# Three projections of a two-layer decoder as three passes over high and low parts

## The chip, the cores and the metric

One core of a Trainium2 chip runs the whole program in one launch. Its engines are TensorE (PE, matrix products), VectorE (DVE), ScalarE (ACT), GpSimd (POOL) and SyncE (SP, which here issues the weight loads); each works off its own instructions in order and waits for the others on semaphores. The metric is the time of one execution on the device, in microseconds (us).

## The reference

Two layers of a causal decoder are computed for 256 prompt tokens and 8 sample tokens (264 columns together), of width 1024, in fp32. What matters here is the head of layer 0:

```python
h = rmsnorm(x, P['norm_mix_pre'][l])
u, v, z, xbc, dt = jnp.split(h @ w_in, SPLIT0, axis=-1)     # widths 1024, 1024, 1024, 1536, 16
u = jax.nn.gelu(u)
v = layernorm(jax.nn.gelu(v), a_ln_g, a_ln_b)
xbc, conv_new = causal_dwconv(xbc, conv0, conv_w, conv_b)   # depthwise, 4 taps
xbc = jax.nn.silu(xbc)
dtf = jax.nn.softplus(dt.astype(f32) + dt_bias.astype(f32))
yb = group_rmsnorm(y * jax.nn.silu(z), b_norm, B_GROUPS)    # y: the scan over xbc with dtf
```

After it come the scan, a spatial gate, the output projection, cross-attention, a dense SwiGLU; then layer 1 with a gated recurrence, cross-attention and eight experts.

## The kernel before

The tokens lie transposed in memory: eight chunks of 128 features by 264 columns (`HT` after a norm). A projection multiplies strips of 512 weight columns; each strip comes in two blocks of four chunks of 128 rows (1 MB), and gives four tiles of 128 outputs by 264 tokens. Blocks are loaded by SyncE (L428 to L433) in the order of the `weights` calls (L350 to L371: xbc, dt, v, z, u, out0, k0, q0 and so on) into a ring of two slots (`RING`); the load of block b waits until block b - 2 is given free. dt has two small blocks of 16 columns.

There are two kinds of projection. The plain one (`project`, L696) multiplies fp32 weights straight from the slot (L712). The split one (`project_split`, L724) takes weights in quarters (two chunks by 512 columns). ScalarE writes a quarter's rounded high part (`make_hi`, L1295), VectorE the rest, its low part (`make_lo`, L1612), both into a ring of four (`QRING`); TensorE then makes three passes: high by high, high by low, low by high (L742 to L744). The tokens have two parts as well: ScalarE writes the high one (`input_hi`, L1316), VectorE the low one within `finish_norm` (L1648 to L1652), for the norms named in `SPLIT_NORMS`. A plain block is free when TensorE has used it, a split one when the low parts of its two quarters are made (L341). A place in the ring of four is free when TensorE has used the quarter.

When the parts are made is set by the order of the instructions on ScalarE and VectorE. Before either takes a finished tile n (`tile`, L1311 on ScalarE and L1628 on VectorE; `copied`, L1633), it makes the parts that tile n needs and up to three (ScalarE) or two (VectorE) quarters beyond:

```python
            goal = needed(n)
            while goal < min(needed(n) + lead, len(quarters)):
                old = quarters[goal][0] - RING
                if old >= 0 and blocks[old][4] is not None and blocks[old][4] > n:
                    break
                goal += 1
            return range(made, max(made, goal))
```

The break is for a quarter whose slot is still held by a plain block. `first_hi`, `first_lo` and `lo_through` make parts at fixed points instead. Four banks take the results in turn, so a new tile waits until the tile four before it is taken out (`take`, L682).

The order on the engines at the head: SyncE loads tokens, parameters and states, then the blocks. TensorE turns the tokens (eight tiles xT), then the parameters and the convolution's state, sums the squares, and goes on with xbc (12 tiles), dt, v (8 tiles), transposes of the convolved xbc, z (8 tiles), the scan. ScalarE squares and copies the eight xT tiles (L1345), makes the root (L1350, `root`), a sigmoid and an exponential of parameters (L1352, L1354), copies xbc's tiles out (L1357), makes an exponential for dt (L1360), waits for VectorE's dt chain, writes two more (L1362), and only then takes v's tiles (L1366); SiLU of xbc (L1369) follows, then z (L1382). VectorE does the norm (`finish_norm(0)`), then the convolution in three groups of four tiles (L1674 to L1696), each when its tiles are out, then a long chain of small operations for dt (L1701 to L1719), and the scan.

Of the kernel before, what the change touches and what calls it, by code (L numbers as in the profile page):

```python
# [21 lines left out]
D = 1024  # L22
DC = D // P
# [39 lines left out]
STEPS_MAX = 3 * NE  # L63


SPLIT = {"q0", "q1", "f", "q", "i", "g"} | {f"{kind}{i}" for kind in ("gate", "up") for i in range(6)}
SPLIT_NORMS = (2, 4, 6, 8)
BIG = 1e30


def program(nc, a, o):
    h_rows = nc.dram_tensor("h_rows", [T, D], F32, kind="Internal").ap()
    oe_rows = nc.dram_tensor("expert_rows", [(STEPS_MAX + 1) * P, D], F32, kind="Internal").ap()
    with ExitStack() as ctx:
# [6 lines left out]
        def S(name):  # L81

            if name not in made:
                made[name] = ctx.enter_context(nc.semaphore(name))
            return made[name]
# [211 lines left out]
        def n_of(name, i=0):  # L297
            return first[name] + i
# [379 lines left out]
        def _(pe):  # L678
# [17 lines left out]
            def project(name, rhs, kchunks, cols, between=None, norm=None):  # L696


                n = n_of(name)
                for c0 in range(0, cols, SL):  # L700
                    width = min(SL, cols - c0)
                    nt = (width + P - 1) // P
                    for k0 in range(0, kchunks, KB):
                        w = next_block()
                        ks = min(KB, kchunks - k0)
                        for i in range(nt):
                            m = min(P, width - i * P)
                            b = take(n + i) if k0 == 0 else bank(n + i)
                            for k in range(ks):
                                if norm is not None and c0 == 0 and i == 0:  # L710
                                    wait_norm(norm, k0 + k + 1)
                                last = mm(b[0:m, 0:T], w[:, k, i * P:i * P + m], rhs[:, k0 + k, :],  # L712
                                          start=(k0 + k == 0), stop=(k0 + k == kchunks - 1))
                            if k0 + ks == kchunks:
                                last.then_inc(tile_done, 1)
                            elif i == nt - 1:
                                last.then_inc(part_used, 1)
                            if between is not None:
                                between()
                    n += nt  # L720
# [81 lines left out]
            pe.wait_ge(S("st_loaded"), 16)  # L802
            transposes(n_of("st"), [(st_in[:, c * P:(c + 1) * P], 24, P) for c in range(CC)])
            square_sums(0)
            project("xbc", HT, DC, CONV_CH, norm=0)
            project("dt", HT, DC, 16)
            project("v", HT, DC, D)

            n = n_of("tr0")
            for i in range(3):  # L810
# [35 lines left out]
            for c in range(DC):  # L846
                last = mm(ps[:, 5, 128 + 16 * c:144 + 16 * c], head_of[:, c * P:(c + 1) * P], exd, start=True, stop=True)
            last.then_inc(S("dt_tm_done"), 1)
            project("z", HT, DC, D)

            b = take(n_of("vmean"))
            pe.wait_ge(empty["a"], emptied(n_of("v", 7))[1])
# [438 lines left out]
        def _(act):  # L1291
# [43 lines left out]
            def root(k):  # L1335
                act.wait_ge(S("square_sums_done"), k + 1)
                f(rs, ps[:, 4, 0:T], ACT.Sqrt, bias=eps_c, scale=1.0 / D).then_inc(S("root_ready"), 1)  # L1337
# [7 lines left out]
            for c in range(DC):  # L1345
                b = tile(n_of("xT", c))
                f(MT[:, c, :], b[:, 0:T], ACT.Square).then_inc(S("squares_ready"), 1)
                f(XT[:, c, :], b[:, 0:T], ACT.Copy).then_inc(empty["a"], 1)
            act.wait_ge(S("eps_ready"), 1)
            root(0)  # L1350
            act.wait_ge(S("lb_diff"), 1)
            f(lb1, omlb, ACT.Sigmoid).then_inc(S("lb_ready"), 1)  # L1352
            act.wait_ge(S("small_loaded"), 64)
# [245 lines left out]
        def _(dve):  # L1599
# [38 lines left out]
            def finish_norm(k):  # L1638

                kind, layer, pre = NORMS[k]  # L1640
                dve.wait_ge(S("root_ready"), k + 1)
                link(v.reciprocal(rs, rs))  # L1642
                if pre:
                    for c in range(DC + 2):
                        if c < DC:
                            STT(out=HT[:, c, :], in0=XT[:, c, :], scalar=gain(kind, layer, c), in1=rs,
                                op0=ALU.mult, op1=ALU.mult).then_inc(S("normed"), 1)
                        if c >= 2 and k in SPLIT_NORMS:  # L1648

                            dve.wait_ge(S("x_hi_made"), DC * SPLIT_NORMS.index(k) + c - 1)  # L1650
                            TT(x_lo[:, c - 2, :], HT[:, c - 2, :], x_hi[:, c - 2, :].bitcast(F32), ALU.subtract) \  # L1651
                                .then_inc(S("x_lo_made"), 1)  # L1652
                else:
                    for c in range(DC + 1):
                        if c < DC:
                            STT(out=MT[:, c, :], in0=MT[:, c, :], scalar=gain(kind, layer, c), in1=rs,
                                op0=ALU.mult, op1=ALU.mult).then_inc(S("out_scaled"), 1)
                        if c:
                            dve.wait_ge(S("out_scaled"), DC * posts.index(k) + c)
                            TT(XT[:, c - 1, :], XT[:, c - 1, :], MT[:, c - 1, :], ALU.add).then_inc(S("x_updated"), 1)  # L1660
# [6 lines left out]
            b = tile(n_of("st"))  # L1667
            v.tensor_copy(raws[:, :, 0:3, :], b[:, 0:288].rearrange("p (c b k) -> p c k b", c=CC, b=NB)) \
                .then_inc(empty["v"], 1)
            finish_norm(0)  # L1670
            dve.wait_ge(S("lb_ready"), 1)
            link(TS(omlb, lb1, -1.0, 1.0, ALU.mult, ALU.add))

            for c4 in range(3):  # L1674
                dve.wait_ge(empty["a"], emptied(n_of("xbc", 4 * c4 + 3))[1])
                cc = range(4 * c4, 4 * c4 + 4)
                for c in cc:
                    last = TS(XBC[:, c, 0:TP], raw[:, c, 3:259], par[:, CW + 36 + c:CW + 37 + c], None, ALU.mult)
                link(last)
                for k in range(3):  # L1680
                    for c in cc:
                        last = STT(out=XBC[:, c, 0:TP], in0=raw[:, c, k:k + TP], scalar=par[:, CW + 12 * k + c:CW + 12 * k + c + 1],
                                   in1=XBC[:, c, 0:TP], op0=ALU.mult, op1=ALU.add)
                    link(last)

                xs = XBC[:, 4 * c4:4 * c4 + 4, TP:T]
                tmp = t2[:, 0, 0:32].rearrange("p (c b) -> p c b", c=4)
                for k in range(4):
                    w = par[:, CW + 12 * k + 4 * c4:CW + 12 * k + 4 * c4 + 4].unsqueeze(2).broadcast_to([P, 4, NB])
                    link(TT(tmp if k else xs, raws[:, 4 * c4:4 * c4 + 4, k, :], w, ALU.mult))  # L1690
                    if k:
                        ins = TT(xs, xs, tmp, ALU.add)
                        if k < 3:
                            link(ins)
                        else:
                            ins.then_inc(S("conv_ready"), 1)  # L1696
# [21 lines left out]
            dve.wait_ge(S("aexp_ready"), 1)  # L1718
            TS(dtr[1], dtr[0], aexp, -1.0, ALU.mult, ALU.mult).then_inc(S("dt_done"), 1)  # L1719

            dve.wait_ge(S("dt_tm_done"), 1)
            v.tensor_copy(small[:, 64:128], ps[:, 5, 0:64]).then_inc(S("dt_tm_ready"), 1)
            link(v.tensor_copy(exc.rearrange("p c k -> p (c k)"), ps[:, 5, 128:256]))
# [449 lines left out]
```

## Time and profile before

| what | us |
|---|---|
| median of three runs | 2319.28 |
| lowest and highest of them | 2318.39, 2330.17 |
| the profiled execution | 2322.26 |
| its span, first to last instruction | 2320.6 |
| TensorE busy in the span | 2115.5 (91%) |
| VectorE busy | 1404.0 (61%) |
| ScalarE busy | 1132.7 (49%) |

The times of single instructions come from the profiled execution, whose time is 2.98 us above the median. In the rows, PE is TensorE's matmuls, PEld its weight loads, DVE VectorE, ACT ScalarE, SPq SyncE's queue; L712 is line 712 of the kernel; "out<-in" names the memory written and read; "xN" is a count; in square brackets stands the idle time before the instruction and what ended it. A plain fp32 product of a 128x128 weight tile shows as two matmul records, each pass of a split one as one. A granted clock of 1.00 is 2.4 GHz, 0.50 is 1.2 GHz.

### The profile page before, as it was taken

Reading aid. Unit: us, or ns where it says so; the run is one execution under the profiler, and the core shown is the slowest. Engines: PE = TensorE matmul, PEld = TensorE weight load, DVE = VectorE, ACT = ScalarE, POOL = GpSimd, SP = SyncE. Lnnn points to the kernel's source line nnn. Section 1 sums busy time; section 2 is a strip of 40 time slices with the busy share of each in tenths; the row PEclk is TensorE's granted clock in tenths of the full one; section 3 lists DMA queues with packets and bytes.
Section 4 is the critical chain, followed back from the end, with each engine's and each line's share of the span. In section 5 each row is a group of like instructions: output and inputs, shape, how many; then the busy total and the mean of one; then the engine's idle time right before and its main releaser. Section 6 shows DMA issues by size and latency. Waiting matters only on the chain.

```text
span 2320.6 us, 28455 instructions
## 1 busy us (share of the span) xinstructions
PE 2115.5 (91%) x10176; PEld 1685.7 (73%) x10176; DVE 1404.0 (61%) x1979; ACT 1132.7 (49%) x1498; POOL 147.4 (6%) x174
## 2 busy tenths in 40 slices
PE   7888789998999877989898699999999999999993
PEld 6675576556998777746656588888888888888882
DVE  2427613423440335371441599999999999999994
ACT  2221213123430235202211478888888888888883
POOL 2002210010000000140010000000000000000001
PEclk9998699999999988769999799999999999999997
DMA  5423354552544464235471599999999999999992
GB/s 134 138 74 100 109 195 150 179 184 91 182 154 146 158 233 134 66 100 205 158 253 55 218 384 369 384 364 386 370 382 368 383 380 374 372 379 376 378 373 74
DMA packets 232760, 551.76 MB, mean 238 GB/s; under 512 B 10406, under 2 KB 13698, under 8 KB 232678
## 3 DMA queue, kind: packets, MB, share of 16 engines
q1 hardware_dynamic: 211246, 470.68, 56.6%
q0 software_dynamic: 21440, 80.07, 10.2%
q8 instruction: 50, 0.82, 0.1%
q14 instruction: 24, 0.20, 0.0%
HBM read 521.18 MB, written 29.62 MB: 237 GB/s over the span
## 4 chain that ended last, share of the span: by engine, by line
PE 79%; DVE 12%; DMA 4%; ACT 3%; issue 2%; POOL 1%; DVEq 0%; ACTq 0%; POOLq 0%
PE banks L712 14%; PE banks L1267 8%; PE banks L1269 8%; PE banks L1268 8%; PE banks L763 5%; PE banks L1260 4%; PE banks L1258 4%; PE banks L1259 4%; PE banks L742 3%; PE banks L743 3%; PE banks L744 3%; PE banks L1049 2%; PE banks L787 2%; PE banks L1017 1%; PE banks L1277 1%
## 5 line engine op out<-in xcount | busy, mean ns | idle before, releaser
L2131 DVE TENSOR_TENSOR weight_parts<-arena,weight_parts 128x1024 fp32r<-128x1024 f32 x672 | 799.5, 1222 | 64.8 <-ACT weight_parts L1567 32.9
L1567 ACT ACTIVATE weight_parts<-arena 128x1024 fp32r<-128x1024 f32 x672 | 702.0, 1062 | 140.1 <-PE banks L1269 89.3
L712 PE MATMUL banks<-arena 128*128 128x264 f32 (+1 forms) x1584 | 372.6, 398 | 19.6 <-DMA arena<-in_ev_w_out 5.1
L712 PEld LDWEIGHTS banks<-arena 128*128 128x128 f32 (+1 forms) x1584 | 308.4, 196 | 83.2 <-issue 9.7
L1267 PE MATMUL banks<-weight_parts,token_parts 128*128 128x512 f32 x896 | 355.9, 397 | 6.2 <-DVE weight_parts L2131 6.2
L1269 PE MATMUL banks<-weight_parts,token_parts 128*128 128x512 f32 x896 | 350.2, 391 | 0.0
L1268 PE MATMUL banks<-weight_parts,token_parts 128*128 128x512 f32 x896 | 349.4, 390 | 0.0
L742 PE MATMUL banks<-token_parts,weight_parts 128*128 128x264 f32 x736 | 218.3, 297 | 47.8 <-DVE token_parts L1651 17.1
L743 PE MATMUL banks<-token_parts,weight_parts 128*128 128x264 f32 x736 | 216.5, 294 | 0.0
L744 PE MATMUL banks<-token_parts,weight_parts 128*128 128x264 f32 x736 | 215.9, 293 | 0.0
L1617 DVE TENSOR_TENSOR weight_parts<-arena,weight_parts 128x1024 fp32r<-128x1024 f32 (+1 forms) x96 | 111.1, 1178 | 154.9 <-ACT weight_parts L1304 138.8
L1267 PEld LDWEIGHTS banks<-weight_parts,token_parts 128*128 128x128 f32 x896 | 168.6, 188 | 42.9 <-DVE weight_parts L2131 9.8
L1269 PEld LDWEIGHTS banks<-weight_parts,token_parts 128*128 128x128 f32 x896 | 168.5, 188 | 35.9
L1268 PEld LDWEIGHTS banks<-weight_parts,token_parts 128*128 128x128 f32 x896 | 168.8, 188 | 33.2
L742 PEld LDWEIGHTS banks<-token_parts,weight_parts 128*128 128x128 f32 x736 | 146.4, 199 | 50.9 <-DVE weight_parts L1617 27.5
L1258 PE MATMUL banks<-weight_parts,token_parts 128*128 128x512 f32 x448 | 175.8, 392 | 0.0
L1260 PE MATMUL banks<-weight_parts,token_parts 128*128 128x512 f32 x448 | 174.6, 390 | 0.0
L1259 PE MATMUL banks<-weight_parts,token_parts 128*128 128x512 f32 x448 | 174.4, 389 | 0.0
L1642 DVE RECIPROCAL arena<-arena 128x264 f32<-128x264 f32 x11 | 19.8, 1801 | 253.9 <-ACT arena L1337 253.6
L1304 ACT ACTIVATE weight_parts<-arena 128x1024 fp32r<-128x1024 f32 (+1 forms) x96 | 96.8, 1022 | 132.9 <-PE banks L744 86.9
L743 PEld LDWEIGHTS banks<-token_parts,weight_parts 128*128 128x128 f32 x736 | 146.3, 199 | 0.0
L744 PEld LDWEIGHTS banks<-token_parts,weight_parts 128*128 128x128 f32 x736 | 145.8, 198 | 0.0
(417 smaller groups left out, 2196.1 us busy)
## 6 DMA issues: line engine op xcount, KB each, us to landing
arena<-in_moe_w_gate SPq DMA_DIRECT2D x112, 1024.0 KB, 7.5
arena<-in_moe_w_up SPq DMA_DIRECT2D x112, 1024.0 KB, 7.8
arena<-in_moe_w_down SPq DMA_DIRECT2D x112, 1024.0 KB, 7.5
arena<-in_ev_w_in SPq DMA_DIRECT2D x18, 1024.0 KB, 5.0
arena<-in_cache_mem_k POOLq DMA_DIRECT2D x16, 1024.0 KB, 6.5
arena<-in_cache_mem_v POOLq DMA_DIRECT2D x16, 1024.0 KB, 7.0
arena<-in_od_w_in SPq DMA_DIRECT2D x16, 1024.0 KB, 5.7
arena<-in_ffn_w_gate SPq DMA_DIRECT2D x10, 1024.0 KB, 5.0
```

Of the source, the lines that this page charges most:

```text
L712: last = mm(b[0:m, 0:T], w[:, k, i * P:i * P + m], rhs[:, k0 + k, :], start=(k0 + k == 0), stop=(k0 + k == kchunks - 1))
L742: mm(b[:, 0:T], hi[:, part], x_hi[:, c, :], start=(c == 0), stop=False)
L743: mm(b[:, 0:T], hi[:, part], x_lo[:, c, :], start=False, stop=False)
L744: last = mm(b[:, 0:T], lo[:, part], x_hi[:, c, :], start=False, stop=(c == DC - 1))
L1258: mm(out, xh, hi[:, cols], start=(s == 0 and i == 0), stop=False)
L1259: mm(out, xh, lo[:, cols], start=False, stop=False)
L1260: last = mm(out, xl, hi[:, cols], start=False, stop=(s == NSL - 1 and i == 3))
L1267: mm(out, xh, hi[:, cols], start=(c == 0), stop=False)
L1268: mm(out, xh, lo[:, cols], start=False, stop=False)
L1269: last = mm(out, xl, hi[:, cols], start=False, stop=(c == DC - 1))
L1567: f(wr_[:, q % QRING, 0, :], quarter(q), ACT.Copy).then_inc(S("hi_made"), 1)
L2131: TT(wr_[:, q % QRING, 1, :], quarter(q), wr_[:, q % QRING, 0, :].bitcast(F32), ALU.subtract) \
```

## The change

xbc, v and z join the split projections (`SPLIT`), and the first norm joins the norms that give both parts (`SPLIT_NORMS`). TensorE calls `project_split` for the three. ScalarE calls `first_hi("xbc")` before the first root and `input_hi(0)` after it. VectorE calls `first_lo("xbc")` before the first norm, `copied` in place of the plain wait ahead of each convolution group, and `lo_through("v", 7, 2)` after dt's chain. dt and u stay plain. With xbc, v and z the list of quarters begins with 28 new ones: 12, 8 and 8, the first four of them in blocks 0 and 1.

```diff
--- before.py
+++ after.py
@@ -63,8 +63,8 @@
 STEPS_MAX = 3 * NE
 
 
-SPLIT = {"q0", "q1", "f", "q", "i", "g"} | {f"{kind}{i}" for kind in ("gate", "up") for i in range(6)}
-SPLIT_NORMS = (2, 4, 6, 8)
+SPLIT = {"xbc", "v", "z", "q0", "q1", "f", "q", "i", "g"} | {f"{kind}{i}" for kind in ("gate", "up") for i in range(6)}
+SPLIT_NORMS = (0, 2, 4, 6, 8)
 BIG = 1e30
 
 
@@ -802,9 +802,9 @@
             pe.wait_ge(S("st_loaded"), 16)
             transposes(n_of("st"), [(st_in[:, c * P:(c + 1) * P], 24, P) for c in range(CC)])
             square_sums(0)
-            project("xbc", HT, DC, CONV_CH, norm=0)
+            project_split("xbc", CONV_CH, norm=0)
             project("dt", HT, DC, 16)
-            project("v", HT, DC, D)
+            project_split("v", D)
 
             n = n_of("tr0")
             for i in range(3):
@@ -846,7 +846,7 @@
             for c in range(DC):
                 last = mm(ps[:, 5, 128 + 16 * c:144 + 16 * c], head_of[:, c * P:(c + 1) * P], exd, start=True, stop=True)
             last.then_inc(S("dt_tm_done"), 1)
-            project("z", HT, DC, D)
+            project_split("z", D)
 
             b = take(n_of("vmean"))
             pe.wait_ge(empty["a"], emptied(n_of("v", 7))[1])
@@ -1346,8 +1346,10 @@
                 b = tile(n_of("xT", c))
                 f(MT[:, c, :], b[:, 0:T], ACT.Square).then_inc(S("squares_ready"), 1)
                 f(XT[:, c, :], b[:, 0:T], ACT.Copy).then_inc(empty["a"], 1)
+            first_hi("xbc")
             act.wait_ge(S("eps_ready"), 1)
             root(0)
+            input_hi(0)
             act.wait_ge(S("lb_diff"), 1)
             f(lb1, omlb, ACT.Sigmoid).then_inc(S("lb_ready"), 1)
             act.wait_ge(S("small_loaded"), 64)
@@ -1667,12 +1669,13 @@
             b = tile(n_of("st"))
             v.tensor_copy(raws[:, :, 0:3, :], b[:, 0:288].rearrange("p (c b k) -> p c k b", c=CC, b=NB)) \
                 .then_inc(empty["v"], 1)
+            first_lo("xbc")
             finish_norm(0)
             dve.wait_ge(S("lb_ready"), 1)
             link(TS(omlb, lb1, -1.0, 1.0, ALU.mult, ALU.add))
 
             for c4 in range(3):
-                dve.wait_ge(empty["a"], emptied(n_of("xbc", 4 * c4 + 3))[1])
+                copied(n_of("xbc", 4 * c4 + 3))
                 cc = range(4 * c4, 4 * c4 + 4)
                 for c in cc:
                     last = TS(XBC[:, c, 0:TP], raw[:, c, 3:259], par[:, CW + 36 + c:CW + 37 + c], None, ALU.mult)
@@ -1718,6 +1721,7 @@
             dve.wait_ge(S("aexp_ready"), 1)
             TS(dtr[1], dtr[0], aexp, -1.0, ALU.mult, ALU.mult).then_inc(S("dt_done"), 1)
 
+            lo_through("v", 7, 2)
             dve.wait_ge(S("dt_tm_done"), 1)
             v.tensor_copy(small[:, 64:128], ps[:, 5, 0:64]).then_inc(S("dt_tm_ready"), 1)
             link(v.tensor_copy(exc.rearrange("p c k -> p (c k)"), ps[:, 5, 128:256]))
```

## Rows read from the trace of the kernel before

**Rows 1.** The page, part 4: the chain that ended last, by engine.

```profile
PE 79%; DVE 12%; DMA 4%; ACT 3%; issue 2%; POOL 1%; DVEq 0%; ACTq 0%; POOLq 0%
```

**Rows 2.** The chain in order of time, 0 to 420 us: start us, us, what.

```profile
22.48 1.28 ACT L1337
...
26.77 46.54 PE banks L712 x200
73.33 5.05 DMA arena<-in_ev_w_in
78.43 30.42 PE banks L712 x128
109.28 1.28 ACT L1369
...
123.28 28.68 PE banks L712 x128
```

**Rows 3.** ScalarE's timeline, 0 to 165 us: start, us, line, operation, count [idle before].

```profile
9.25 0.39 ACT L1347 ACTIVATE arena<-banks 128x264 f32<-128x264 f32 x1 [7.03 <-PE banks L778]
...
14.99 0.39 ACT L1347 ACTIVATE arena<-banks 128x264 f32<-128x264 f32 x1
...
24.28 1.28 ACT L1352 ACT_TABLE_LOAD   x1
...
71.45 0.38 ACT L1357 ACTIVATE arena<-banks 128x256 f32<-128x256 f32 x1 [1.33 <-PE banks L712]
...
89.82 0.21 ACT L1362 ACTIVATE arena<-arena 16x8 f32<-16x8 f32 x1 [8.21 <-DVE arena L1719]
```

**Rows 4.** Loads of L433: the first alone, then the first two.

```profile
DMA to landing us min/median/max: 5.1/5.1/5.1
...
L433 SPq DMA_DIRECT2D arena<-in_ev_w_in x2: 394/451/508, 8.0 to 8.4; - x2
...
DMA to landing us min/median/max: 5.1/11.4/17.7
```

**Rows 5.** Stretches: us, granted clock, share of DMA engines, GB/s.

```profile
13.00:21.70 8.70, 1.00 0.66 25
```

**Rows 6.** VectorE's timeline, 0 to 165 us.

```profile
71.94 1.14 DVE L1678 TENSOR_SCALAR arena<-arena 128x256 f32<-128x256 f32 x4 [6.40 <-ACT arena L1358]
...
79.70 0.18 DVE L1698 COPY arena<-arena 128x36 f32<-128x36 f32 x1
```

**Rows 7.** A norm that gives both parts (before q0): VectorE, TensorE, ScalarE, in time.

```profile
395.90 1.80 DVE L1642 RECIPROCAL arena<-arena 128x264 f32<-128x264 f32 x1
...
399.53 0.56 PE L742 MATMUL banks<-token_parts,weight_parts 128*128 128x264 f32 x1 [4.18 <-DVE token_parts L1651]
...
402.81 0.43 ACT L1320 ACTIVATE token_parts<-arena 128x264 fp32r<-128x264 f32 x1 [0.32 <-DVE arena L1646]
```

**Rows 8.** Parts of q0's weights: ScalarE's and VectorE's timelines.

```profile
403.14 2.94 ACT L1304 ACTIVATE weight_parts<-arena 128x1024 fp32r<-128x1024 f32 x3
...
404.22 3.49 DVE L1617 TENSOR_TENSOR weight_parts<-arena,weight_parts 128x1024 fp32r<-128x1024 f32 x3 [0.41 <-ACT weight_parts L1304]
```

**Rows 9.** ScalarE's timeline: the copies of q0's last four tiles, first and last.

```profile
422.93 0.39 ACT L1447 ACTIVATE arena<-banks 128x264 f32<-128x264 f32 x1 [8.10 <-PE banks L744]
...
425.12 0.39 ACT L1447 ACTIVATE arena<-banks 128x264 f32<-128x264 f32 x1 [0.34 <-PE banks L744]
```

**Rows 10.** Stretches: us, TensorE busy (x), granted clock, DMA share, GB/s.

```profile
75.40:78.40 3.00, 0.00 (x0) 1.00 1.05 383
78.40:80.00 1.60, 1.57 (x4) 0.50 1.15 324
80.00:82.00 2.00, 2.00 (x7) 0.55 1.05 385
```

**Rows 11.** The page, part 5: weight loads of a split line; busy us, mean ns.

```profile
L742 PEld LDWEIGHTS banks<-token_parts,weight_parts 128*128 128x128 f32 x736 | 146.4, 199 | 50.9 <-DVE weight_parts L1617 27.5
```

**Rows 12.** The page, part 6: DMA issues of a line, KB, us to landing.

```profile
arena<-in_moe_w_gate SPq DMA_DIRECT2D x112, 1024.0 KB, 7.5
```

## Prediction

> **What bounds the kernel now.** I began with the shares of the chain that ended last: TensorE has 79% of the span, so a matmul that gets shorter is worth looking at [rows 1]. Then the same chain in order of time, over the stretch that the change touches [rows 2]: nearly all of 26.77 to 151.96 us is L712, the plain fp32 projections. xbc runs from 26.77 to about 71.45, when ScalarE takes its last tile [rows 3]; dt follows, then the load that ends at 78.38 [rows 2]; v takes 30.42 us and z 28.68 us. The stage is TensorE's, with VectorE and ScalarE largely idle beside it. So the question is whether these two, which now must make every weight's two parts, do it in time. Their queues are in order, and I read the order from the code.
>
> **The matmul itself: a gain.** z's 64 products (8 tiles of 8 chunks) took 28.68 us, 0.448 each [rows 2]. In the projections that are split already, four tiles end within 422.93 to 425.12 us, so a tile's last six matmuls (two chunks, three passes) take 0.73 us [rows 9], and a quarter of a weight strip (two chunks by 512 columns), 24 matmuls, takes 2.92 us. xbc, v and z are 12, 8 and 8 quarters: 28 x 2.92 = 81.8 us, against 44.7 (26.77 to 71.45) + 30.4 + 28.7 = 103.8 now. Alone that is 22 us of gain. A rule speaks against it: the Trainium skill (Perfetto Trace Analysis, Identifying the Most-Contended Engine) judges TensorE by the time of its weight loads and not of its matmuls. If loads were the bound, three at the 199 ns that a load is shown with [rows 11] make 0.60 us a product, and 224 products would lose 33 us; but three passes fit in 0.365 us [rows 9], so the loads overlap and I keep the matmuls' rate.
>
> **The start: +17.4 us.** The ScalarE helper that takes a finished tile (`tile`, L1311) first makes the high parts of up to three quarters beyond those needed (`ahead_of`, L377). Before the change the first quarters belonged to q0, whose ring slot is held by an earlier plain block, and the loop broke off. Now the first three belong to blocks 0 and 1, no block was before them, and ScalarE makes all three before its very first square; the `first_hi` that the change adds then finds nothing left. Block 0 lands 5.1 us after 8.0, at 13.1; the largest of the first two landings is 17.7, so block 1, issued at 8.4, lands at 26.1 [rows 4]. Between 13 and 21.7 us the queues moved 25 GB/s [rows 5]. Quarter 2 lies in block 1, so its conversion (1.06 us on ScalarE) ends at 27.2, and behind it wait all squares and copies of the tokens, the root and the table loads. The first square now stands at 9.25, the last at 14.99 [rows 3]. TensorE has four transposed tiles ready (four banks), the other four follow at 0.82 us each (14.99 - 9.25 over seven) from 27.9, when the first bank is free: the last is turned at 31.2, 16.2 later than now. The rest up to the root is TensorE's own and moves along: root's table load at 38.7 instead of 22.48 [rows 2]. The norm then also gives the low part: where it is already done so, TensorE starts 3.63 us after the reciprocal's start [rows 7]; so root (1.8 with its table: ScalarE is at its next table load at 24.28 [rows 3]), then 40.5 + 3.63 = 44.15 instead of 26.77.
>
> **xbc: +7.3 us.** ScalarE's high part takes 1.06 (2.94 for three), VectorE's low part 1.2 (3.49 for three) [rows 8]. Each strip of four tiles adds a convolution of 7.8 us on VectorE (71.94 to 79.70) [rows 6], in which no low part is made. Working through it: ScalarE ends the token parts 7.3 us after the reciprocal began (402.81 + 0.43 against 395.90) [rows 7], then come two table loads of 1.28 with an operation each (3.0; the first is shown [rows 3]): quarter 3's parts are ready at 51.9 and 53.1. Quarters 0 to 3 run 44.15 to 57.5, with 1.7 us for a clock that starts low: after the 3 us gap of now, 75.4 to 78.4, 0.50 was granted and then 0.55 until 82, the lower level of 1.2 GHz [rows 10], and 3.6 us at half speed lose some 1.7. SyncE now reloads a slot on the low parts' count: block 3 goes out at 53.1 and lands 5.05 later [rows 2] at 58.2. ScalarE asks for its first half (quarter 6) before it empties the first tile, so that bank is free at 59.8 and not right after the tile, at 55.9. Quarters 4 and 5 run 59.8 to 66.8 (1.2 for the clock). The fourth tile is out at 61.25, the convolution ends at 69.05, the low part of quarter 6 at 70.25: 3.5 us of idle, then 6 and 7 until 77.85 (again 1.7). Block 5 goes out on quarter 7's low part, 71.4, and lands at 76.45; quarters 8 and 9 run 78.05 to 83.9. The second convolution, 79.5 to 87.3, puts quarter 10's low part at 88.5: 10 and 11 run 88.55 to 96.1. That is 51.95 us where 44.68 were.
>
> **dt and the wait before v: +14.0 us.** dt stays plain and takes 3.9 us as now (71.45 to 75.4, where TensorE falls idle [rows 10]): 96.1 to 100. The look-ahead stops at dt's plain blocks, so ScalarE first makes a high part of v after it has written dt's exponentials, for which it waits on VectorE: third convolution, then the dt chain. From the third convolution's start at 71.94 [rows 6] to ScalarE's going on behind the chain at 89.82 [rows 3] are 17.9 us now. TensorE doesn't wait for it there, only for v's load. After: 96.6 + 17.9 = 114.5, two short operations 0.3, high part 1.06, low part 1.2: v starts at 117.1 instead of 78.43. What is late next, were this gone, is v's block (issued when half of dt is done, 98, landed 103), so the load is hidden.
>
> **v and z: -5.3 and -5.3 us.** v's eight quarters: 23.4 plus 1.7 for the clock, 25.1 against 30.4. The conversions stay ahead: 1.2 of VectorE and 1.06 of ScalarE to 2.92 of TensorE, and the blocks go out two quarters earlier than they are used. Between v and z (the SiLU of the convolution, transposes, 109.28 to 123.28 [rows 2]) nothing changes. z's first two quarters are made during v; 23.4 against 28.7. u is plain and its loads go out earlier. GpSimd's queue waits for the same events as now.
>
> **Sum.** 17.4 + 7.3 + 14.0 - 5.3 - 5.3 = +28.1 us. The profiled execution took 2322.26 us (span 2320.6), 2.98 above the median of 2319.28; so it would be 2350.4 for such an execution and **2347** for the median.
>
> **Bounds.** Block 1's landing: one load's time (5.05) after block 0, at 18.2, gives back 7.9 us; at 15.2, when ScalarE has made the first two quarters, the most, 10.9; block 2, which now goes out at 16.5, can push it to the end of the burst, some 2 us later. I take 26.1, since block 2 is behind it in one queue. The loads on the path (blocks 3 and 5): 5.05 to the 7.5 us of the expert weights [rows 12], +5. The clock: no loss after the three gaps within xbc (-4.6) or twice the loss (+4.6). Token parts and table loads are rows of their own and move little.
>
> **Rivals.**
> 1. The cover holds: every low part is ready when TensorE asks. It decides at the point where VectorE's low part of quarters 6, 10 and 12 comes before the quarter ahead has ended, and it needs ScalarE not to stand still at the start. Then 103.8 becomes 81.8, and only the norm costs 1.1 (1.8 + 3.63 where 22.48 to 26.77 is 4.29 now): 2298. For it: VectorE and ScalarE have the time in total. Against: the order of their queues. Chance 0.03. The Trainium skill (FP8 and Floating Point Precision, TensorE Precision Notes) has true fp32 as four passes, so three would save a quarter, an estimate of 26 us of 103.8; the trace doesn't quite agree, 0.365 to 0.448 is 19%.
> 2. Block 1 is not late, since the slow interval of 13 to 21.7 moves: +18 instead of +28, 2337. For it: it is one interval of one execution. Against: the small loads that fill it are issued as before. 0.12.
> 3. As 2, and the stalls in xbc are half of mine: 2319 + 28 - 10 - 6 = 2331 or less, about the edge of no change. 0.05.
> 4. The loads on the path at 7.5 us, clock low for longer: 2358 to 2364. 0.12.
> 5. Weight loads bind, as the rule has it: 33 us lost and 22 not gained in the matmuls, partly in time that is idle in the forecast: from 2347 to some 2390. 0.02.
>
> The forecast has the remaining 0.66, at 2341 to 2356.
>
> **How the numbers follow.** Rival 2 and the lower end of rival 4 belong in the range: 2334 to 2359; outside are 1, 3, 5 and the upper part of 4, below 0.2. 0.5% is 11.6 us, about what a measurement of this kernel can tell from no change: faster (under 2307.7) 0.03, within 0.5% 0.05, slower 0.92.
>
> **What would show it.** In the changed profile: ScalarE's first instructions are three of L1304, the third waiting until about 26 us for a load, and the first square behind them. The first split matmul near 44. In xbc two idle times of TensorE before L742 that end on VectorE's L1617, each after a convolution (L1682). A gap of some 17 us after dt, closed by the chain L1714, ScalarE's exponentials, L1304, L1617. v in about 25 us, z in about 23.4, and everything after z as it was, 28 us later. If the first square is still near 9 us, the first step is wrong; if TensorE goes on to v before dt's exponentials are written, the third is.

## The result, and the profile after

| what | before | after |
|---|---|---|
| median, us | 2318.84 (4 runs, 2315.7 to 2330.17) | 2343.86 (4 runs, 2341.69 to 2349.34) |
| the profiled execution, us | 2322.26 | 2341.69 |
| its span, us | 2320.6 | 2340.1 |

The ratio is 1.0103, with a 95% interval of 1.0064 to 1.0141: 25 us slower, where the forecast was 28 (2347, range 2334 to 2359). TensorE's share of the chain that ended last fell from 79% [rows 1] to 75%: its matmuls did get shorter, and other engines took their place on the path. The interval is wide, 14.8 to 32.7 us. Line numbers of after lie up to four above those of before, and those of the experiments up to some seven higher still.

ScalarE's timeline of after, 0 to 165 us: start, us, line, operation, count, and in brackets the idle time before it and what ended it ("..." stands for lines left out).

```profile
13.11 2.00 ACT L1304 ACTIVATE weight_parts<-arena 128x1024 fp32r<-128x1024 f32 x2 [10.90 <-DMA arena<-in_ev_w_in]
25.32 1.06 ACT L1304 ACTIVATE weight_parts<-arena 128x1024 fp32r<-128x1024 f32 x1 [10.20 <-DMA arena<-in_ev_w_in]
26.28 0.37 ACT L1347 ACTIVATE arena<-banks 128x264 f32<-128x264 f32 x1
...
94.90 0.38 ACT L1359 ACTIVATE arena<-banks 128x256 f32<-128x256 f32 x1 [0.27 <-PE banks L744]
...
113.26 0.21 ACT L1364 ACTIVATE arena<-arena 16x8 f32<-16x8 f32 x1 [8.21 <-DVE arena L1722]
113.48 3.88 ACT L1304 ACTIVATE weight_parts<-arena 128x1024 fp32r<-128x1024 f32 x4
```

ScalarE's first work is three high parts (L1304). The third stands still for 10.20 us until block 1 lands at 25.3, and the first square, at 9.25 before [rows 3], comes behind it at 26.28. At the other end, the first high part of v waits for the exponential at 113.26.

TensorE's timeline of after, the entries that begin with an idle time, from the first split matmul to the scan.

```profile
43.71 0.56 PE L742 MATMUL banks<-token_parts,weight_parts 128*128 128x264 f32 x1 [5.53 <-DVE token_parts L1653]
59.30 0.36 PE L742 MATMUL banks<-token_parts,weight_parts 128*128 128x264 f32 x1 [2.32 <-ACT arena L1360]
69.27 0.39 PE L742 MATMUL banks<-token_parts,weight_parts 128*128 128x264 f32 x1 [2.35 <-DVE weight_parts L1619]
77.31 0.36 PE L742 MATMUL banks<-token_parts,weight_parts 128*128 128x264 f32 x1 [0.42 <-ACT arena L1360]
87.26 0.39 PE L742 MATMUL banks<-token_parts,weight_parts 128*128 128x264 f32 x1 [3.88 <-DVE weight_parts L1619]
115.83 0.59 PE L742 MATMUL banks<-token_parts,weight_parts 128*128 128x264 f32 x1 [17.30 <-DVE weight_parts L1619]
142.31 1.47 PE L814 MATMUL banks<-arena 128*11 128x128 f32 x12
...
180.14 3.72 PE L854 MATMUL banks<-arena 128*128 128x264 f32 x16
```

Read from the top this is the whole case: the first matmul 17 us late, four small idle times in xbc (two end on a low part, L1619), one of 17.30 us before v, and then v and z, which run faster than before. L854, the first work behind z, began at 151.8 before (the row below has the first and the last of its 16 starts); the shift there is 28.3 us.

```profile
L854 PE MATMUL banks<-arena x16: 386/386/386, 151.8 to 155.1; 128*128 128x264 f32 x16
```

Stretches of after: us, TensorE busy (and matmuls), granted clock, share of the DMA engines, GB/s. They are xbc's first and last piece after an idle time, the gap before v, v's start, the rest of v, and z.

```profile
43.70:48.00 4.30, 4.29 (x24) 0.64 0.01 4
...
87.20:95.00 7.80, 7.74 (x49) 0.78 0.05 6
98.70:115.70 17.00, 0.00 (x0) 0.58 0.43 148
115.70:119.00 3.30, 3.17 (x14) 0.50 0.25 52
119.00:142.60 23.60, 23.52 (x183) 0.94 0.59 201
156.80:180.20 23.40, 23.40 (x193) 1.00 0.42 135
```

Most pieces that follow an idle time ran in part at the lower level of the clock: those shown, and two more of xbc, granted 0.78 each (59.30 to 66.90 and 69.20 to 77.00 us). xbc's piece behind the idle time of 0.42 us was granted 1.00, and so was z, which follows the transposes without one.

### The profile page after: what moved, and what is told of

The parts are those of the page before. It is cut to its first block, busy times and chain, and to the rows that moved or that the text cites. A ratio compares the mean times of both kernels' runs of the same rounds, so it can differ in the third digit from the quotient of the medians.

```text
span 2340.1 us, 29004 instructions
## 1 busy us (share of the span) xinstructions
PE 2098.1 (90%) x10400; PEld 1684.3 (72%) x10400; DVE 1442.0 (62%) x2015; ACT 1162.3 (50%) x1534; POOL 148.3 (6%) x174
## 4 chain that ended last, share of the span: by engine, by line
PE 75%; DVE 14%; DMA 5%; ACT 4%; issue 2%; SPq 0%; POOL 0%; DVEq 0%; ACTq 0%; POOLq 0%
PE banks L712 9%; PE banks L1267 8%; PE banks L1269 8%; PE banks L1268 8%; PE banks L763 5%; PE banks L1260 4%; PE banks L1258 4%; PE banks L1259 4%; PE banks L742 4%; PE banks L743 4%; PE banks L744 4%; PE banks L1049 2%; PE banks L787 2%; PE banks L1017 1%; DMA arena<-in_ev_w_in 1%
## 5 line engine op out<-in xcount | busy, mean ns | idle before, releaser
L742 PE MATMUL banks<-token_parts,weight_parts 128*128 128x264 f32 x960 | 285.6, 298 | 76.9 <-DVE weight_parts L1619 27.3
L743 PE MATMUL banks<-token_parts,weight_parts 128*128 128x264 f32 x960 | 282.9, 295 | 0.0
L744 PE MATMUL banks<-token_parts,weight_parts 128*128 128x264 f32 x960 | 282.5, 294 | 0.0
L712 PE MATMUL banks<-arena 128*128 128x264 f32 (+1 forms) x1136 | 266.6, 397 | 13.4 <-DMA arena<-in_ev_w_out 6.3
L712 PEld LDWEIGHTS banks<-arena 128*128 128x128 f32 (+1 forms) x1136 | 219.7, 195 | 59.5 <-DMA arena<-in_ev_w_out 6.7
L1619 DVE TENSOR_TENSOR weight_parts<-arena,weight_parts 128x1024 fp32r<-128x1024 f32 (+1 forms) x124 | 146.1, 1202 | 181.8 <-ACT weight_parts L1304 166.0
L742 PEld LDWEIGHTS banks<-token_parts,weight_parts 128*128 128x128 f32 x960 | 191.6, 200 | 82.2 <-DVE weight_parts L1619 50.3
L1304 ACT ACTIVATE weight_parts<-arena 128x1024 fp32r<-128x1024 f32 (+1 forms) x124 | 125.8, 1030 | 188.1 <-PE banks L744 105.1
L743 PEld LDWEIGHTS banks<-token_parts,weight_parts 128*128 128x128 f32 x960 | 191.3, 199 | 0.0
L744 PEld LDWEIGHTS banks<-token_parts,weight_parts 128*128 128x128 f32 x960 | 190.7, 199 | 0.0
L1258 PE MATMUL banks<-weight_parts,token_parts 128*128 128x512 f32 x448 | 175.8, 392 | 0.0
```

The lines of the kernel that those rows point to most:

```text
L742: mm(b[:, 0:T], hi[:, part], x_hi[:, c, :], start=(c == 0), stop=False)
L743: mm(b[:, 0:T], hi[:, part], x_lo[:, c, :], start=False, stop=False)
L744: last = mm(b[:, 0:T], lo[:, part], x_hi[:, c, :], start=False, stop=(c == DC - 1))
L1258: mm(out, xh, hi[:, cols], start=(s == 0 and i == 0), stop=False)
```

## The experiments

The theory: the loss is made of three waits that the order of ScalarE's and VectorE's queues sets (the start, the low parts behind the convolutions, v's parts behind dt's chain), and the matmuls themselves gain. The main rival: that the split passes are not worth having here. Experiments 1, 2 and 5 each take on one wait by the order alone, e4 asks what held block 1, e3 and e8 split fewer projections, e6 takes all three waits away. In each the marks are the start of xbc, of v, and of the first work behind z (L854, "z's end").

**e1_start.** The look-ahead makes nothing before xbc's own tiles (in `ahead_of`):

```diff
+            if n < first["xbc"]:
+                return range(0)
             while goal < min(needed(n) + lead, len(quarters)):
```

> The changed kernel, with ScalarE and VectorE kept from making weight parts before the first tile of xbc (the look-ahead returns nothing there), so that the added first_hi and first_lo make two quarters. Theory of the order (the time is lost because the conversions stand ahead of other work in the in-order queues): the first square is back at about 9.3 us instead of 26.3, the root's table load at 22.5 instead of 38.3, the first split matmul near 28 instead of 43.7; quarter 2's parts then come 1 to 2 us late, so 14 to 16 us of the 25 come back, about 2329 us. Theory of the amount (the conversions cost by what they add to ScalarE and VectorE, wherever they stand): only the third high part is saved before the root, at most 3 us, about 2341.

Measured: 2329.0 us (8 runs), ratio 1.0041 (1.0027 to 1.0055). ScalarE's timeline, then TensorE's:

```profile
9.24 0.39 ACT L1349 ACTIVATE arena<-banks 128x264 f32<-128x264 f32 x1 [7.03 <-PE banks L780]
...
15.54 2.00 ACT L1306 ACTIVATE weight_parts<-arena 128x1024 fp32r<-128x1024 f32 x2
```

```profile
28.35 0.56 PE L744 MATMUL banks<-token_parts,weight_parts 128*128 128x264 f32 x1 [5.52 <-DVE token_parts L1655]
...
101.18 0.59 PE L744 MATMUL banks<-token_parts,weight_parts 128*128 128x264 f32 x1 [17.30 <-DVE weight_parts L1621]
```

The squares are back at 9.24 and the same two high parts follow them, from data that has landed by then. xbc starts 15.4 us earlier than in after; the waits in xbc stay (and one of 1.60 us on a low part is new, at 37.43), and so do the 17.30 before v. z's end moves from 180.1 to 165.0. The start is shown to be a cause of its own, worth 15 us.

**e4_small_loads.** GpSimd issues its loads, small ones of parameters and 1 MB of states, only when block 1 has landed; nothing else is changed, so ScalarE still converts first:

```diff
+            pool.wait_ge(loaded[1], 16)
             for j in range(2):
                 g.dma_start(dcol[64 * j:64 * j + 64, :],
```

> The changed kernel, with GpSimd's small parameter loads and its state loads issued only when the second weight block has landed. If block 1 comes at 25 us because these loads hold the DMA engines between 13 and 21.7 us, it now lands by 16 to 19 us, the first square is at 17 to 20 instead of 26.3, and 7 to 9 us come back, about 2336. If block 1 is late of itself, its landing and the time stay, 2344.

Measured: 2336.0 us (4 runs), ratio 1.0057 (1.004 to 1.0074). ScalarE's timeline, then TensorE's, then the times from issue to landing of the first two weight blocks, then a stretch (columns as above):

```profile
15.98 1.06 ACT L1305 ACTIVATE weight_parts<-arena 128x1024 fp32r<-128x1024 f32 x1 [0.64 <-DMA arena<-in_ev_w_in]
16.95 0.37 ACT L1348 ACTIVATE arena<-banks 128x264 f32<-128x264 f32 x1
```

```profile
34.83 0.56 PE L743 MATMUL banks<-token_parts,weight_parts 128*128 128x264 f32 x1 [5.53 <-DVE token_parts L1654]
```

```profile
DMA to landing us min/median/max: 5.3/6.4/7.5
```

```profile
16.00:21.70 5.70, 4.05 (x16) 1.00 0.72 0
```

Block 1 lands 7.5 us after its issue; in after it took 16.9. The stretch of 16.00 to 21.70, now behind the block, shows the DMA engines 72% busy at 0 GB/s: 16 packets of GpSimd's queue that move next to nothing. In before, [rows 5] had them in front of the block at 25 GB/s. xbc starts at 34.83, 8.9 us earlier than in after, and z ends 7.8 us earlier. So the start's 17 us are mainly two things: some 9 for block 1 behind GpSimd's loads, and some 6.5 (34.83 against 28.35 in e1_start) for conversions ahead of the squares even when the block is prompt. Of the last 1.6 (28.35 against 26.77) the norm with both parts is 1.15 (5.44 from the root's table load to the first matmul, 4.29 before), and the rest is a root that began 0.4 later, less than the 0.6 between the two profiles of before. The edit doesn't part the small loads from the states: in after 32 packets of GpSimd's queue took 73% of the DMA engines' time from 16 to 21.7 us, and from 21.7 to 25.3 it moved 0.44 MB, of states by the size, beside SyncE's 0.80.

**e2_v_first.** v's first strip is converted on both engines before dt's chain instead of behind it:

```diff
+            make_hi(range(12, 16))
             act.wait_ge(S("dt_abs_ready"), 1)
...
             v.tensor_scalar(x_, b[0:16, 0:T], dtb, None, ALU.add).then_inc(empty["v"], 1)
+            make_lo(range(12, 16))
```

> The changed kernel, with the first four quarters of v converted ahead of dt's chain: ScalarE makes the high parts before dt's exponential, VectorE the low parts right after the first operation of the chain. Theory of the order: TensorE starts v when its block has landed and one quarter is converted, near 105.5 us instead of 115.8; the chain (10 us) then runs beside v's first strip, and ScalarE comes some 2 us late with quarter 16; 7 to 9 us come back, about 2336. Theory of the amount: the same operations are done, the chain only ends later (4.8 us), and v's tiles wait for ScalarE behind it: nothing gained, 2343 to 2348.

Measured: 2344.94 us (4 runs), ratio 1.0101 (1.0085 to 1.0118). TensorE's timeline, then ScalarE's:

```profile
105.22 0.59 PE L742 MATMUL banks<-token_parts,weight_parts 128*128 128x264 f32 x1 [6.49 <-DVE weight_parts L1620]
124.38 0.36 PE L742 MATMUL banks<-token_parts,weight_parts 128*128 128x264 f32 x1 [4.62 <-ACT arena L1369]
```

```profile
102.21 2.00 ACT L1304 ACTIVATE weight_parts<-arena 128x1024 fp32r<-128x1024 f32 x2 [6.66 <-DMA arena<-in_ev_w_in]
...
119.39 0.21 ACT L1365 ACTIVATE arena<-arena 16x8 f32<-16x8 f32 x1 [8.20 <-DVE arena L1724]
...
119.60 2.93 ACT L1304 ACTIVATE weight_parts<-arena 128x1024 fp32r<-128x1024 f32 x3
122.55 1.28 ACT L1369 ACT_TABLE_LOAD   x1
123.85 1.24 ACT L1369 ACTIVATE arena<-banks 128x264 f32<-128x264 f32 x4
```

In the time a miss: 2344.94 is what the theory of the amount had (2343 to 2348), in part for its reason, since v's tiles wait for ScalarE behind the chain. In the head half a miss: v starts 10.6 us earlier, and what is late there now is v's load, as the prediction named it next. But the second strip needs a free bank, and ScalarE takes v's first tile out only at 123.85: behind dt's exponential (119.39), three high parts and a table load. z's end moves by 4.3 us only, not the 7 to 9 expected. The profiled execution has them (2337.71 against 2341.69), but it is the fastest of four that range to 2346.85, and the median shows no gain at all. Moving a conversion past a wait is not enough while the copies that free the banks stay behind that wait.

**e5_between.** VectorE makes single low parts between the steps of the first two convolutions:

```diff
                 for k in range(3):
+                    if c4 < 2 and k != 1:
+                        make_lo([lo_count[0]])
```

> The changed kernel, with the low parts of the next two quarters made within xbc's first and second convolutions (one ahead of the first tap's sum, one ahead of the third) and not behind them. Theory of the order: the two idle times of TensorE in xbc that end on a low part after a convolution (2.4 and 3.9 us) go, with the low clock after them and the late loads of block 5 behind quarter 7's low part; xbc ends 8 to 11 us earlier, about 2335 us. Theory of the amount: the convolution gets longer by what the low parts take (2.4 us each time) and the tiles behind it wait for that: within 2 us of the changed kernel. Theory of the loads (xbc is bound by SyncE's reloads, which now wait on low parts): idle times move to the loads, and less than 3 us come back.

Measured: 2336.56 us (4 runs), ratio 1.0068 (1.0047 to 1.009). TensorE's timeline, all idle times from 40 us to the scan, then stretches of it:

```profile
45.15 0.56 PE L742 MATMUL banks<-token_parts,weight_parts 128*128 128x264 f32 x1 [5.52 <-DVE token_parts L1653]
60.55 0.36 PE L742 MATMUL banks<-token_parts,weight_parts 128*128 128x264 f32 x1 [1.80 <-ACT arena L1360]
74.89 0.36 PE L742 MATMUL banks<-token_parts,weight_parts 128*128 128x264 f32 x1 [2.42 <-ACT arena L1360]
109.28 0.59 PE L742 MATMUL banks<-token_parts,weight_parts 128*128 128x264 f32 x1 [17.30 <-DVE weight_parts L1619]
```

```profile
142.00:146.00 4.00, 4.00 (x19) 0.50 0.10 17
146.00:150.00 4.00, 4.00 (x31) 0.77 0.02 4
150.00:155.00 5.00, 5.00 (x30) 0.66 0.00 0
```

Both idle times that ended on a low part are gone, and xbc to v is 8.0 us shorter (109.28 - 45.15 against 115.83 - 43.71), so those waits came of low parts that stood behind the convolutions. xbc began 1.4 us later here, so v starts 6.55 us earlier than in after, and the transposes 7.25; at z's end only 4.6 us are left: the transposes and z's first part, with the same instructions and the same idle time before them (5.45 us, against 5.46 in after), were granted 0.50 to 0.77 for the 13 us from their start, where after had 0.57 for the first 4 us (149 to 153) and 1.00 behind them.

**e3_z_only.** Only z is split (`SPLIT` without xbc and v, `first_hi("xbc")` and `first_lo("xbc")` left out, `first_lo("z")` behind dt's chain); the first norm gives both parts as in after.

> Only z is split (xbc and v plain, as before the change), with the first norm giving both parts; z's first two quarters are made during v. Theory of the order: no stall at the start, none before v, z takes 23.4 us instead of 28.7, the norm with its token parts costs up to 1 us: 4 to 5 us less than the kernel before, about 2314. Theory of the amount: 8 high and 8 low parts on engines that are idle there cost nothing either, so this run tells the gain by itself: if a split strip of 264 columns isn't worth 5 us in 8 quarters, z ends less than 3 us earlier and the time is that of the kernel before.

Measured: 2312.63 us (10 runs), ratio 0.9973 (0.9957 to 0.9988). The time came out as expected, but not for the reason given. TensorE's timeline, the idle times before z:

```profile
79.68 30.44 PE L712 MATMUL banks<-arena 128*128 128x264 f32 x128 [3.01 <-DMA arena<-in_ev_w_in]
116.88 1.11 PE L822 MATMUL banks<-arena 128*128 128x128 f32 x4 [5.46 <-ACT arena L1370]
120.20 2.82 PE L822 MATMUL banks<-arena 128*128 128x128 f32 x12 [2.20 <-ACT arena L1326]
```

z itself is 64 products from 127.5 on, and ends at 152.5 where before ended at 151.8 and b_again, the second profile of before (below), at 153.0: v starts 1.25 us later than in before (0.15 than in b_again), ScalarE makes three of z's high parts (116.73, for 2.93) before it empties the transposes' banks (the 2.20), and z's first matmuls run in part at the lower clock (0.77 granted from 125 to 130 us). The gain of z is used up before z is over. In the profile the time that this kernel is shorter by arose behind z, where it runs the same instructions as before (2159.5 us, against 2168.8 and 2165.6); the 7 us of the medians are not shown to be z's.

**e8_v_z.** xbc plain; v and z split, with v's parts made early as in e2_v_first and three more high parts ahead of the wait for dt's chain:

```diff
+            make_hi(range(0, 4))
             act.wait_ge(S("dt_abs_ready"), 1)
             f(dtr[3], dtr[3], ACT.Exp, scale=-1.0).then_inc(S("dt_exp_ready"), 1)
+            make_hi(range(4, 7))
             act.wait_ge(S("dt_done"), 1)
```

> v and z split, xbc plain, with v's first strip converted ahead of dt's chain as in the run with all three moves. If xbc's own split is worth little even with all moves made (there it ran from 28.1 to 71.0 us, 42.9 where the plain one took 44.7, and the norm with both parts costs 1.3), this kernel ends z at 146 to 149 us, as that one (147.1), and takes 2308 to 2314 us. If xbc's split is worth its share of the matmul time (96 of 224 products, some 8 us), z ends at 152 to 155 and the time is 2316 to 2320.

Measured: 2318.09 us (12 runs), ratio 0.9999 (0.9989 to 1.0008): a miss in the time. The head did as expected, v starts at 81.24 and z ends at 149.1, 2.7 us before where it did; the time shows none of that. That a gain of this size reaches the end is not to be relied on. Against e6_all (147.1), which has xbc split as well, z ends 2 us later: in these two profiles xbc's own split is worth 2 us at z's end even with all moves made, not its share of 8.

**e6_all.** The edits of e1_start, e2_v_first and e5_between together, and `make_hi(range(16, 19))` ahead of the wait for dt's chain, so that the copies come right behind dt's exponentials.

> All three moves together: no conversion before xbc's first tile, low parts within the convolutions, v's first strip converted ahead of dt's chain, and here the high parts of quarters 16 to 18 made while ScalarE waits for that chain, so that v's first tiles are taken out right after it. Theory of the order: z ends 15 + 10 + 7 us before the changed kernel, at 146 to 150 us, and the time is 2308 to 2314, below the kernel before (2319). Theory of the amount: no lower than the first move alone, 2329.

Measured: 2314.81 us (12 runs), ratio 0.9974 (0.996 to 0.9989). TensorE's timeline, idle times to the transposes:

```profile
28.10 0.56 PE L744 MATMUL banks<-token_parts,weight_parts 128*128 128x264 f32 x1 [5.53 <-DVE token_parts L1657]
37.18 0.39 PE L744 MATMUL banks<-token_parts,weight_parts 128*128 128x264 f32 x1 [1.69 <-DVE weight_parts L1623]
44.88 0.36 PE L744 MATMUL banks<-token_parts,weight_parts 128*128 128x264 f32 x1 [1.59 <-ACT arena L1362]
59.17 0.36 PE L744 MATMUL banks<-token_parts,weight_parts 128*128 128x264 f32 x1 [2.39 <-ACT arena L1362]
...
81.22 0.59 PE L744 MATMUL banks<-token_parts,weight_parts 128*128 128x264 f32 x1 [6.49 <-DVE weight_parts L1623]
97.35 0.36 PE L744 MATMUL banks<-token_parts,weight_parts 128*128 128x264 f32 x1 [2.26 <-ACT arena L1372]
```

z ends at 147.1:

```profile
L856 PE MATMUL banks<-arena x16: 385/386/387, 147.1 to 150.4; 128*128 128x264 f32 x16
```

That is 33 us earlier than in after and 4.7 earlier than in before (5.9 than in b_again). The same three passes on the same weights, with the conversions in another order, turn a loss of 28 us at z's end into a gain of 4.7, and in the medians a loss of 25 into a gain of 4 (0.1 to 0.4%). So the rival, that the passes are no use here, falls at z's end. That the 4 us at the end are the same gain is not shown: e3_z_only gained 7 there with nothing at z's end, e8_v_z none with 2.7. The gain is small all the same: of the 22 us that the matmuls alone promise, the five waits inside the projections and before v take 14.4 again (1.69 + 1.59 + 2.39 + 6.49 + 2.26, of which the plain xbc and v had 3 before v), and the norm 1.15. Of the 9.5 us then left, 4.7 came; stretches at the lower clock (0.63 from 28.1 to 32.0 us, 0.84 from 81.2 to 95.0) took a part of the rest, which is not accounted for in full.

**b_again and a_again.** The kernels before and after once more, one execution each, to see what repeats behind z.

> The kernel before once more, for a second profile. From z's last matmul to the end the first profile has 2168.8 us, the changed kernel's 2160.0. If this part varies from execution to execution, the second profile differs from the first by several us; if it is a matter of the program, it gives 2168 to 2169 again.

> The changed kernel once more, for a second profile. The head of the program is set by its queues: first square at 25 to 27 us, first split matmul at 43 to 45, v at 115 to 117, z's end at 179 to 182. From there to the end: 2160 again if it is a matter of the program, 2155 to 2170 if it varies from execution to execution.

Measured: 2320.22 and 2341.49 us. Times between the first matmuls of chosen lines of the plain program behind z (us; worked out from the start times in the traces), L1177 and L1189 being the two ends of layer 1's first cross-attention:

| from, to | before | b_again | after | a_again |
|---|---|---|---|---|
| z's end (L854) to L909, the scan | 46.6 | 46.6 | 45.7 | 45.6 |
| L909 to L985, spatial gate, u, out0 | 121.4 | 121.4 | 119.1 | 119.0 |
| L985 to L1139 | 633.9 | 634.0 | 632.4 | 632.4 |
| L1139 to L1177 | 78.6 | 78.6 | 77.9 | 77.9 |
| L1177 to L1189 | 252.5 | 248.2 | 249.0 | 248.9 |
| L1189 to the end | 1035.8 | 1036.8 | 1035.9 | 1035.6 |

The first four repeat to 0.2 us: after is 5.4 to 5.6 us shorter there, in instructions that the change doesn't touch. The fifth doesn't repeat in before (252.5 and 248.2) and belongs to the execution. Two pairs of rows locate some 3 of the 5.5 us: the stretch of out0 that follows a wait of 2.45 us in both kernels (columns as above; b_again, then a_again),

```profile
308.75:311.75 3.00, 3.00 (x7) 0.50 0.69 270
```

```profile
334.29:337.29 3.00, 3.00 (x14) 1.00 0.69 262
```

and the wait of ScalarE for the load of f's weights in layer 1 (ScalarE's timeline, before, then after).

```profile
825.90 1.06 ACT L1304 ACTIVATE weight_parts<-arena 128x1024 fp32r<-128x1024 f32 x1 [12.44 <-DMA arena<-in_od_w_in]
```

```profile
850.86 1.06 ACT L1304 ACTIVATE weight_parts<-arena 128x1024 fp32r<-128x1024 f32 x1 [10.99 <-DMA arena<-in_od_w_in]
```

The same wait, and the clock fell in the one and not in the other: 7 records against 14 in 3 us, 1.5 us. The load is 1.45 us less late. Both are so in the two other profiles too (0.50 in before and 1.00 in after; 12.55 us in b_again and 11.04 in a_again). Why, stays open. It isn't what the change computes: e4_small_loads has the whole change, and its first two segments are 47.0 and 121.8, above those of before. z's end and the time behind it in all profiles (us):

| run | z's end | from there to the end of the span |
|---|---|---|
| before, b_again | 151.8, 153.0 | 2168.8, 2165.6 |
| after, a_again | 180.1, 180.5 | 2160.0, 2159.4 |
| e1_start | 165.0 | 2159.8 |
| e2_v_first | 175.8 | 2160.3 |
| e3_z_only | 152.5 | 2159.5 |
| e4_small_loads | 172.4 | 2166.5 |
| e5_between | 175.6 | 2160.1 |
| e6_all | 147.1 | 2159.7 |
| e8_v_z | 149.1 | 2169.2 |

The part behind z is near 2160 in seven profiles and 2166 to 2169 in four, and it doesn't follow the head: up to 9 us, twice the gain of e6_all. Moves of z's end by 15 or 28 us are clear of that in the total time; moves by 2 to 8 us are safely read at z's end only.

## Why the prediction was right, step by step

**The start: right** (+17.4 forecast, 43.71 - 26.77 = +16.9 measured, +16.75 in the second pair of profiles). Its marks: block 1 landed 26.1 forecast and 25.3 measured, the first square 27.2 and 26.28, the root's table load 38.7 and 38.26. Its cause, ScalarE standing in front of a block that is late, is shown by e1_start and e4_small_loads. That the slow stretch of [rows 5] is small loads was only supposed there; e4_small_loads shows it, since the stretch moves with them.

**xbc: right in kind, one term too large** (+7.3 forecast, 94.90 - 43.71 - 44.68 = +6.5 measured). Both idle times behind a convolution are there, of 2.35 and 3.88 us. The first was put at 3.5: the fourth tile was out a microsecond earlier than I had it (the convolution began at 60.22, 61.25 in the forecast), and quarters 4 and 5 took 7.6 us where I had 7.0. The second, which I had at 4.6 (88.55 - 83.9), is 0.8 shorter as well. How the time parts among the waits is a matter of the execution: a_again has 0.82 on the copy and 3.88 behind the first convolution where after has 2.32 and 2.35, the same sum, and its xbc is +6.8. The two short idle times that end on ScalarE's copy (2.32, 0.42) were forecast by their mark, quarter 6's conversion ahead of the copy: 59.8 forecast, 59.30 measured.

**dt and the wait before v: right** (+14.0 forecast; 115.83 - 94.90 = 20.9 where 78.43 - 71.45 = 7.0 were, +13.9). The chain is the one named: the exponential at 113.26, a high part at 113.48, its low part, v at 115.83. That v's load is next was also right (e2_v_first, e6_all: 6.49 us of idle, and ScalarE waiting for the load).

**v and z: z right, v mis-sized.** z took 23.4 as forecast. v took 26.5 (115.83 to 142.31), where 25.1 was the forecast: I had the lower clock for the first 3.6 us only, and it lasted for 6.2: 0.50 until 119 us, 0.52 from there to 122, then 1.00. So the stretch from 119 us on had 0.94 on average, 6% of 23.6 us, the missing 1.4.

**The matmul itself: right.** z's 64 products in 23.40 us are 0.366 us each, against 0.365 forecast and 0.448 plain [rows 2]. The Trainium skill (Perfetto Trace Analysis, Identifying the Most-Contended Engine) has TensorE judged by its share of the peak arithmetic and by the busy share of its weight loads, not by matmul time; taken as a bound, as in rival 5, the loads would have given 0.60. Here the trace doesn't agree: 0.366, though a weight load is still shown with 200 ns. The Trainium skill (FP8 and Floating Point Precision, TensorE Precision Notes) has true fp32 as four passes, so three would take 0.336, an estimate; 0.366 is what the trace has.

**"Everything after z as it was, 28 us later": wrong.** At z's end the shift was 28.3 us in the first pair of profiles and 27.5 in the second. Between there and L1177 after was some 5.5 us quicker, twice, and it ended 19.5 us later in the first pair, 21.3 in the second and 25.0 by the medians. For such an execution the forecast was 2350.4, and 2341.69 was measured: all of these 8.7 us lie behind z. By the medians the miss is 3 us, less than their interval can tell from none. I had counted every instruction behind z by its duration before; the granted clock and how long a load waits are not properties of an instruction.

**Luck.** The sum for the head, +28.1, meets the 28.3 at z's end better than its terms do: the start, xbc and the wait were 0.5, 0.8 and 0.1 us too high, and v 1.4 too low, which cancels. The mechanism of each term was seen, and all but v's are within 1 us; that the sum comes so close is partly chance.

**The rivals.** Rival 2 (the block isn't late) describes e4_small_loads: 2337 worked out, 2336.0 measured. Rival 1 (the cover holds, 2298) is what e6_all aims at; it reached 2314.8, since the waits for banks and for v's load stay. Rival 3 didn't occur: block 1 was late, and xbc's idle times were most of those forecast. Of rival 4 the loads are out: blocks 3 and 5 were there at 57.8 and 75.8, where 58.2 and 76.45 were forecast. A longer low clock, its other half, cost 1.4 us in v and 0.6 in quarters 4 and 5. Rival 5 (weight loads bind) is out by z's 23.4.

## What to carry to other kernels

A faster matmul that needs its operands prepared by other engines is worth what their in-order queues allow: walk each queue from the top, and ask of every prepared piece what stands behind it (here all squares of the tokens, behind one late load) and what it stands behind (v's parts, behind a chain for dt that v's matmuls don't need). Fix the order before judging the passes: at z's end the same passes lost 28 us in one order and gained 4.7 in another. A gain of some microseconds at the head is only a gain once the time at the end shows it, and a gain at the end is the head's only if the head shows it too.

## What the runs showed that I had not expected

- The DMA engines can be 72% busy at 0 GB/s (16.00 to 21.70 us in e4_small_loads), and a 1 MB block took 16.9 us to land behind such loads and GpSimd's states, where 7.5 sufficed without them.
- The same idle time ahead of the same instructions can leave the clock at 1.00 or at 0.50 (out0 after 2.45 us), or at the lower level for 4 us or in part for 13 (the transposes and z after 5.46 us in after and 5.45 in e5_between), worth 1.5 and 2.7 us. So part of what a step saves can go, or more can come, at a place that it doesn't touch.
